# The scan phase of a two-block kernel: a loop over heads rewritten as staggered, unrolled periods

## The reference, cut to what matters

```python
def _gla_chunked(q, k, v, logf, s0):
    ...
    bc = jnp.cumsum(logf, axis=3)                       # within a chunk
    ref = bc[..., CHUNK // 2:CHUNK // 2 + 1, :]
    scores = jnp.einsum('bhnid,bhnjd->bhnij', q * jnp.exp(bc - ref), k * jnp.exp(ref - bc))
    scores = jnp.where(incl, scores, 0.0)
    o_intra = jnp.einsum('bhnij,bhnjv->bhniv', scores, v)
    q_dec = q * jnp.exp(bc)
    k_dec = k * jnp.exp(bc[..., -1:, :] - bc)
    tot = jnp.exp(bc[..., -1, :])
    def step(S, xs):                                    # over the chunks
        o_c = jnp.einsum('bhcd,bhdv->bhcv', qd_c, S)
        S = tot_c[..., :, None] * S + jnp.einsum('bhcd,bhcv->bhdv', kd_c, v_c)
    ...
# around it, per head: q = silu(q), f = lb + (1 - lb) * sigmoid(fx), logf = log(f), k = 1 - f,
# o = rmsnorm(o_forward + flip(o_backward)) * norm_w * silu(gate)
```

## Time and profile before

| | us |
|---|---|
| median of three executions | 5560.26 |
| profiled execution, its own time | 5562.48 |
| its span | 5560.7 |
| scan phase in it | 448.40 |
| TensorE busy in the scan phase | 232.37 |
| VectorE busy in the scan phase | 252.79 |
| ScalarE busy in the scan phase | 171.10 |

### The profile page before, as it was taken

How to read it: one execution, slowest core, us unless ns; L and a number is a source line. 1 busy time by engine, 2 the same in 40 slices (tenths; PEclk the granted TensorE clock), 3 DMA queues, 4 the chain that set the end, 5 groups by cost and what they waited for, 6 DMA issues and landing times. The chain is left out here.

```text
span 5560.7 us, 68785 instructions
## 1 busy us (share of the span) xinstructions
PE 4873.5 (88%) x24244; PEld 3969.3 (71%) x24244; DVE 3176.1 (57%) x5103; ACT 2093.4 (38%) x2408; POOL 110.1 (2%) x167
## 2 busy tenths in 40 slices
PE   8927799999999389997999954568999999899998
PEld 3923487778777278885899944433788888788887
DVE  0062498889888622232888746522787666344444
ACT  1001277776767201112555534310333444322222
POOL 1000100000000100000000011000000000000000
PEclk9557899999999789998999955579999999999999
DMA  8402599999999432344011011032434445566663
GB/s 337 151 30 89 228 369 366 365 368 370 367 363 368 154 134 106 109 145 124 29 35 35 15 43 42 30 108 92 148 126 132 168 171 198 193 210 192 192 195 122
DMA packets 256044, 976.04 MB, mean 176 GB/s; under 512 B 27060, under 2 KB 63492, under 8 KB 202212
## 3 DMA queue, kind: packets, MB, share of 16 engines
q1 hardware_dynamic: 248516, 923.74, 46.4%
q0 software_dynamic: 7392, 50.50, 2.2%
HBM read 799.87 MB, written 174.28 MB: 175 GB/s over the span
## 5 line engine op out<-in xcount | busy, mean ns | idle before, releaser
L84 PE MATMUL peer_bank<-peer_t_high,peer_high 128*128 128x512 f32 x2176 | 856.4, 394 | 49.3 <-DVE peer_low L2662 35.3
L86 PE MATMUL peer_bank<-peer_t_high,peer_low 128*128 128x512 f32 x2176 | 849.7, 390 | 0.0
L85 PE MATMUL peer_bank<-peer_t_low,peer_high 128*128 128x512 f32 x2176 | 848.2, 390 | 0.0
L2662 DVE TENSOR_TENSOR peer_low<-peer_raw,peer_high 128x1024 fp32r<-128x1024 f32 x272 | 332.4, 1223 | 621.8 <-ACT peer_high L3003 621.8
L1076 DVE TENSOR_TENSOR moe_low<-moe_raw,moe_high 128x2048 fp32r<-128x2048 f32 x256 | 574.4, 2285 | 55.9 <-ACT moe_high L984 53.0
L84 PEld LDWEIGHTS peer_bank<-peer_t_high,peer_high 128*128 128x128 f32 x2176 | 409.8, 188 | 133.0 <-issue 50.5
L984 ACT ACTIVATE moe_high<-moe_raw 128x2048 fp32r<-128x2048 f32 x256 | 478.0, 1905 | 2.6 <-DMA moe_raw<-w_gate_up 2.6
L86 PEld LDWEIGHTS peer_bank<-peer_t_high,peer_low 128*128 128x128 f32 x2176 | 409.5, 188 | 86.7
L3003 ACT ACTIVATE peer_high<-peer_raw 128x1024 fp32r<-128x1024 f32 x272 | 287.1, 1056 | 489.6 <-PE peer_bank L86 481.5
L85 PEld LDWEIGHTS peer_bank<-peer_t_low,peer_high 128*128 128x128 f32 x2176 | 410.0, 188 | 83.6
L1081 DVE TENSOR_TENSOR moe_low<-moe_raw,moe_high 128x2048 fp32r<-128x2048 f32 x128 | 292.9, 2288 | 66.8 <-ACT moe_high L989 66.8
(11 more groups left out here) (537 smaller groups left out, 9356.0 us busy)
## 6 DMA issues: line engine op xcount, KB each, us to landing
moe_raw<-w_gate_up SPq DMA_DIRECT2D x256, 1024.0 KB, 6.8
moe_raw<-w_down SPq DMA_DIRECT2D x128, 1024.0 KB, 7.4
peer_raw<-expert_u SPq DMA_DIRECT2D x128, 512.0 KB, 3.7
peer_raw<-expert_v SPq DMA_DIRECT2D x128, 512.0 KB, 3.6
hidden<-peer_gelu SPq DMA_DIRECT2D x128, 256.0 KB, 2.1
gate_matrix<-peer_stage SPq DMA_DIRECT2D x8, 4096.0 KB, 12.1
peer_stage<-gate_matrix SPq DMA_DIRECT2D x32, 1024.0 KB, 7.5
peer_stage<-hidden SPq DMA_DIRECT2D x128, 256.0 KB, 3.4
```

Of the source, the lines that this page charges most:

```text
L84: pe.matmul(out, wh, xh, start=start, stop=False)
L85: pe.matmul(out, wh, xl, start=False, stop=False)
L86: return pe.matmul(out, wl, xh, start=False, stop=stop)
L2662: v.tensor_tensor(low_part[:, slot], raw[:, slot], high[:, slot].bitcast(F32), ALU.subtract).then_inc(cut_low, 1)
```

## The change

In the input phase ScalarE's copies are unrolled, and those of the 40 tiles that the scan phase reads (two forget inputs, i, q, gate of the branch) write the 512 grid tokens in column order, reading PSUM with a stride of 64 elements. The scan phase has no such reordering left, nor any work of GpSimd after its start.

In the scan phase the loop is unrolled into periods p = -1 to 9. In period p the engines do three things in turns: the start of head p+1 (sigmoid, q, v, log, cumulative sums), the middle of head p (decays, scores, updates, states), and the end of heads p-1 (output, sum of squares, gate, logarithm) and p-2 (inv, o1, o2). Tiles q and v have two buffers. The tiles of the two directions lie in one tile with a direction axis, so that Sigmoid, Ln, e1 to e4, k, kd, ke, qe and qd are one instruction for both. The mask is a predicated copy of the whole bank (pt, `visible`), qd moves to VectorE (`queries`), and root and reciprocal give way to Ln (lno) and Exp (inv) on ScalarE. `Marks` is `Steps` with the head's number known when the code is made.

```diff
-            def copy_only(i, n, ps):
+            def in_order(tile, dst, src):
+
+                if tile // HEADS in (Z_FF // HEADS, Z_FB // HEADS, Z_I // HEADS, Z_QB // HEADS, Z_GB // HEADS):
+                    return by_columns(dst), src.rearrange("p (r w) -> p w r", w=GRID_W)
...
+                act.activation(*in_order(tile, out[:, n, 0:SEQ], bank[n % 2][0][:]), ACT.Copy).then_inc(half_taken, 1)
+                act.wait_ge(half_taken, tile + 1)
+                act.activation(out[:, n, SEQ:], bank[n % 2][1][:], ACT.Copy).then_inc(both.taken, 1)
...
-
-            def body(i):
-                for n in range(4):
-                    act.wait_ge(both.products, i * 4 + n + 1)
-                    need(act, z_stored[n], 16 * i)
-                    act.activation(out[:, n, 0:SEQ], bank[n % 2][0][:], ACT.Copy).then_inc(half_taken, 1)
-                    act.wait_ge(half_taken, i * 4 + n + 1)
-                    act.activation(out[:, n, SEQ:], bank[n % 2][1][:], ACT.Copy).then_inc(both.taken, 1)
-
-            rounds(act, BOTH // 4, body)
-            only.take(act, copy_only)
...
-        fz = [s.sb(f"fz{r}", [P, TOK]) for r in dirs]
+        fz = s.sb("fz", [P, 2, TOK])
...
+        q = [s.sb(f"q{n}", [P, SEQ]) for n in range(2)]
+        v = [s.sb(f"v{n}", [P, PAIRS, P]) for n in range(2)]
+        sg, k, lf, bc, dl, e4, kd = (s.sb(n, [P, 2, TOK]) for n in ("sg", "k", "lf", "bc", "dl", "e4", "kd"))
+        dm, e1, e2, e3, qe, ke, qd = (s.sb(n, [P, 2, SEQ]) for n in ("dm", "e1", "e2", "e3", "qe", "ke", "qd"))
...
+            def log_out(h):
+                TO.after(act, "sumsq", h)
+                VE.after(act, "o1", h - 1)
+                AO.mark("lno", h, act.activation(inv[:], ssb[:], ACT.Ln, scale=DK_SCALE ** 2, bias=eps[:]))
+
+            for p in PERIODS:
+                if head(p - 2):
+                    AO.after(act, "lno", p - 2)
+                    AE.mark("inv", p - 2, act.activation(inv[:], inv[:], ACT.Exp, scale=-0.5))
+                if head(p):
+                    decays(p, ("e4", "e2", "e1", "tot_f", "tot_b"))
+                    keys(p, 0)
+                    decays(p, ("e3",))
+                    keys(p, 1)
+                if head(p - 1):
+                    square_out(p - 1)
+                if head(p + 1):
+                    sigmoids(p + 1)
+                if head(p - 1):
+                    gates(p - 1)
+                if head(p + 1):
+                    values(p + 1)
+                    logs(p + 1)
+                if head(p - 1):
+                    log_out(p - 1)
...
+            def outputs(h):
+                VE.after(pe, "o1", h - 1)
+                AO.after(pe, "sq", h - 1)
+                VS.after(pe, f"s{NCH - 2}_b", h)
                 for r in dirs:
...
+                        pe.matmul(ob[:, c * P:(c + 1) * P], v[h % 2][:, c], pt[r][:, c], start=r == 0 and c == 0, stop=False,
                                   skip_group_check=True)
...
+                        last = pe.matmul(ob[:, part], state[r][:, c], qd[:, r, part], start=False, stop=r == 1,
                                          skip_group_check=True)
-            rounds(pe, HEADS, body)
+                TO.mark("out", h, last)
...
+            for p in PERIODS:
+                if head(p):
+                    turn_keys(p, 0)
+                    scores(p, 0)
+                if head(p - 1):
+                    outputs(p - 1)
+                if head(p):
+                    turn_keys(p, 1)
+                    updates(p, 0)
+                    scores(p, 1)
+                    updates(p, 1)
+                if head(p - 1):
+                    sums(p - 1)
+                if head(p + 1):
+                    turn_values(p + 1)
...
-            def body(h):
...
+            def lengths(h):
+                AG.after(ve, "sg", h)
+                VS.after(ve, "ke", h - 1)
+                VG.mark("k", h, ve.tensor_scalar(k[:], sg[:], lbm1[:, h:h + 1], oml[:, h:h + 1], ALU.mult, ALU.add))
...
-                    for b, (lo, part) in enumerate(windows[r]):
-                        rows = slice(lo, lo + 32)
-                        m = mask[r][rows, part].unsqueeze(1).to_broadcast([32, 4, part.stop - part.start])
-                        V.mark(f"pt{b}_{x}", ve.tensor_tensor(pt[r][rows, :, part], ptb[rows, :, part], m, ALU.mult))
...
-                V.mark("meansq", ve.tensor_scalar(root[:], ssb[:], DK_SCALE ** 2, RMS_EPS, ALU.mult, ALU.add))
-                A.after(ve, "root", h)
-                V.mark("inv", ve.reciprocal(inv[:], root[:]))
...
+                    order = (lambda a: a) if r == 0 else (lambda a: a[:, ::-1])
+                    AG.after(ve, "lf", h)
+                    AS.after(ve, "e3", h - 1)
+                    VG.mark(f"bc_{x}", h, ve.tensor_tensor_scan(order(bc[:, r]), keep[:], order(lf[:, r]), 0.0, ALU.mult, ALU.add))
...
+            def decayed(h):
+                AS.after(ve, "e4", h)
+                VG.after(ve, "k", h)
+                TS.after(ve, "tk1_b", h - 1)
+                VS.mark("kd", h, ve.tensor_tensor(kd[:], k[:], e4[:], ALU.mult))
...
+            def visible(h, r):
+                x = R[r]
+                TS.after(ve, f"scores_{x}", h)
+                TO.after(ve, "out", h - 1)
+                VS.mark(f"pt_{x}", h, ve.copy_predicated(pt[r][:], mask[r][:].unsqueeze(1).to_broadcast([P, 4, P]).bitcast(U32), ptb[:]))
+
+            def queries(h):
+                AS.after(ve, "e3", h)
+                TO.after(ve, "out", h - 1)
+                VS.mark("qd", h, ve.tensor_tensor(qd[:], q[h % 2][:].unsqueeze(1).to_broadcast([P, 2, SEQ]), e3[:], ALU.mult))
...
-            rounds(ve, HEADS, body)
...
+            for p in PERIODS:
+                if head(p - 2):
+                    norm(p - 2)
+                if head(p):
+                    decayed(p)
+                if head(p - 2):
+                    gated(p - 2)
+                if head(p):
+                    visible(p, 0)
+                    queries(p)
+                    states(p, 0)
+                    visible(p, 1)
+                if head(p + 1):
+                    lengths(p + 1)
+                if head(p):
+                    states(p, 1)
+                if head(p + 1):
+                    sums_of_logs(p + 1)
```

More of the change, by code:

```diff
@@ new lines, in sigmoids, with values, logs @@
+                AG.mark("q", h, act.activation(q[h % 2][:], qz[:], ACT.Silu))
+            def values(h):
+                TO.after(act, "out", h - 2)
+                for n, (a, b) in enumerate(spans):
+                    TG.after(act, f"tv{n}", h)
+                    AG.mark(f"v{n}", h, act.activation(v[h % 2][:, a:b], tr[n][:, 0:b - a], ACT.Copy))
+            def logs(h):
+                act.wait_ge(lbs, 3)
+                VG.after(act, "bc_b", h - 1)
+                AG.after(act, "sg", h)
+                AG.mark("lf", h, act.activation(lf[:], sg[:], ACT.Ln, scale=oml[:, h:h + 1], bias=lb[:, h:h + 1]))
@@ new lines, in gates @@
+            def gates(h):
+                act.wait_ge(loaded["g"], 16 * (h + 1))
+                VE.after(act, "o2", h - 1)
+                AO.mark("gate", h, act.activation(gate[:], gz[:], ACT.Silu))
+            def log_out(h):
[22 more added lines that the diff above has]
+                    log_out(p - 1)
@@ new lines, in turn_keys, with turn_values @@
+                        last = pe.transpose(tr[n][:, c - a], kd[:, r, c * P:(c + 1) * P], ident[:])
+                    TS.mark(f"tk{n}_{R[r]}", h, last)
+            def turn_values(h):
+                pe.wait_ge(loaded["i"], 16 * (h + 1))
+                for n, (a, b) in enumerate(spans):
+                    AS.after(pe, f"kdt{n}_b", h - 1)
+                    for c in range(a, b):
+                        last = pe.transpose(tr[n][:, c - a], iz[:, c * P:(c + 1) * P], ident[:])
+                    TG.mark(f"tv{n}", h, last)
@@ new lines, in scores @@
+            def scores(h, r):
+                x = R[r]
+                VS.after(pe, "qe", h)
+                if r:
+                    VS.after(pe, "pt_f", h)
+                else:
+                    VS.after(pe, "pt_b", h - 1)
+                for c in range(4):
+                    for lo, part in windows[r]:
+                        last = pe.matmul(ptb[lo:lo + 32, c, part], ke[:, r, c * P + lo:c * P + lo + 32],
+                                         qe[:, r, c * P + part.start:c * P + part.stop], start=True, stop=True)
+                TS.mark(f"scores_{x}", h, last)
@@ new lines, in updates @@
+            def updates(h, r):
+                x = R[r]
+                AS.after(pe, f"kdt1_{x}", h)
+                AG.after(pe, "v1", h)
+                if r:
+                    VS.after(pe, f"s{NCH - 2}_f", h)
+                else:
+                    VS.after(pe, f"s{NCH - 2}_b", h - 1)
+                for n in range(2):
+                    if n:
+                        TS.after(pe, f"kv0_{x}", h)
+                    for c in range(n, NCH, 2):
```

(17 more changed lines are left out.)

305 lines of the change are left out of this document (130 added, 175 removed).

## The result

| kernel | median, us | lowest to highest | runs | ratio to before [95%] |
|---|---|---|---|---|
| before | 5560.92 | 5558.92 to 5561.85 | 4 | |
| changed | 5470.8 | 5466.23 to 5480.48 | 4 | 0.9841 [0.9824, 0.9858] |
| predicted | 5475.0 | 5440 to 5520 | | |

The changed kernel is 90 us faster, 4 us more than forecast. The first view is the table of stretches of the changed kernel (columns as in the earlier trace rows). Its rows are, in this order: the scan phase, its period 4, in that period the backward updates and then the stretch from within the outputs to the recurrence, and last period 0.

A forecast was written before the change was run, and what follows sets the result against it. Scan phase bound by a chain of waits through all engines, not by one engine: 19.3 + 35.3 + 252 + 56 = 362.6 us against 448.4, so 5560.3 - 85.8 + 0.5 = 5475 us, range 5440 to 5520.

The forecast's parts named there:

- e4: ScalarE in the scan phase: one decay instruction for both directions, 1536 elements, priced at 1.5 us.
- start, to the end of the first sums: Scan phase start: first lf left at 11 us, then lf 1.65 and cumulative sums 6.6, together 19.3 us.
- periods 1 to 6: Scan phase: 48.3 us a period at 1.2 GHz, less 2.6, 2.8 and 0.8 for the clock, gives 42.
- end: Period 7 without sums: its outputs done at 45.8 us, then 10 to the end of the phase: 56 us.
- input phase: Strided copies of 40 tiles near 1.1 us, hidden except once at the change between lists: 0.5 us more.
- The chain: Scan phase bound by a chain across engines and heads; v and Ln of head p+1 stand behind all of head p.
- The waits named: Expected idle: TensorE some 14 us before kd's transposes, VectorE about 5 before the first state copy and 3 before sums.
- The clock: TensorE rises to 2.4 GHz within or just after the outputs, is down again for backward kv: 42 us a period.
- the two rivals on it: Clock down all through: 5517 us, chance 0.17; clock up for most of each period: 5412 to 5441, chance 0.14.
- the period nearer 35.6: Scan period walked with TensorE at 2.4 GHz from the outputs on: 35.6 us, taken as the skill page's rule.
- The prices: Instruction times in the scan phase from earlier rows: kd 1.75, sigmoid 1.5, Ln 1.65, pt 0.73 us.
- The rival in which this made the kernel slower: Input phase: strided PSUM reads make ScalarE the bound; with 12 us a copy 5675 us, chance 0.02.

The follow-up runs named there:

- the waits filled: Changed kernel plus unread matmuls of 128x512 in TensorE's waits, ten before the forward transposes and three before the backward updates: 5438.82 us.
- six extra matmuls: Kernel with the outputs behind the updates plus 6 unread matmuls of 128x512 before the forward transposes of each head: 5413.91 us.

## Why the prediction was right

Its terms, measured in the profiled execution (a period's length is the same from kd's transposes as from the end of the sums, 3.4 us earlier):

| term | predicted | measured |
|---|---|---|
| start, to the end of the first sums | 19.3 | 19.2 |
| period 0 | 35.3 | 35.8 |
| periods 1 to 6 | 6 x 42 = 252 | 250.3 (43.2, 43.8, 40.8, 40.7, 40.9, 40.9) |
| end | 56 | 53.5 |
| phase | 362.6 | 358.8 |
| input phase | +0.5 | none |

**The chain.** It was the right one, and the experiments moved two of its links: v ahead of the last updates took 15 to 19 us off, and with the outputs out of the way of the forward updates as well it was 47 to 51 (by the two medians of the changed kernel). VectorE's own 23 us a period never became the bound. The waits named are there: TensorE 13.5 us for kd (about 14), VectorE 1.95 before the first state copy (about 5, the part that was too large, since kv came earlier at 2.4 GHz) and 2.38 before the sums (about 3).

**The clock.** It rose within the outputs and was down for the backward updates, as forecast, and in this profile the two rivals on it fell: it was neither down throughout nor up for most of a period (0.61 on the mean). Inside that step the sizes were off. The outputs, taken at 8.5 us, took 9.0 and 9.6 in periods 1 and 2, where the clock rose late in them, and 6.6 to 6.8 in periods 3 to 6. The backward kv, taken at 5.1 although the same sentence had the clock down for it, took 5.88 like every other kv at 1.2 GHz. So two periods were over 43 and four under 41, and that their sum lies within 2 us of 6 x 42 is partly luck. The step itself had luck too: with only qd moved to GpSimd, three periods in one execution took 47.9 us, near the 48.3 of the rival in which the clock stays down. state x qd at 2.4 GHz, for which there was no row, takes 1.73 to the next start; 1.8 was used.

The prediction has the period nearer 35.6 by the rule of the Trainium skill ("TensorE: Matmul & The Clock Gate", Part 1). That reads only half of it: the same part has the clock back at its low level after idling, and the trace agrees, since it is at 0.50 behind the waits for kd (13.5 us) and for the recurrence (3.73). So 35.6 is a walk at full clock and not what the page gives. As such a walk it is good: with the waits filled the one period that kept the high clock nearly throughout took 35.2 us. Four others took 37.4 to 37.9; in period 3 the sum of squares and v's transposes are 2.07 and 1.46 us instead of 1.12 and 0.82, 1.6 us of the difference.

**The prices** held: kd of 1536 1.76 us (1.75), e4 1.48 (1.5), sigmoid 1.49 (1.5), Ln 1.67 (1.65), pt 0.73. For Ln the slope of its own rows gives 1.75 (1.94 less a fixed part of 0.19), so the 1.65 is a lucky figure. Ln starts 0.02 us behind its table load again (3433.07 + 1.28 = 3434.35, and 3434.37), and the load 0.02 us behind the copies of v, so the drain of 1.38 us in the Trainium skill ("ScalarE: Activation LUTs", What ACT_TABLE_LOAD costs) isn't there in this case either.

**The start and the end.** The phase came out 3.8 us short, 2.5 of them at the end. The forecast has the backward kv of period 7 at 31 us, which its own terms don't give (34.9 - 2.6 - 2.8 - 0.8 = 28.7); it was there at 27.6. Against that, from the last square to the end of the phase it was 11.3 us for 10: the gate's load and Silu and the load for Ln lie in it, and the forecast had left them out.

**The input phase.** The strided read costs nothing: 24 of the first 40 copies and 16 of the other 48 are strided, and both groups are as long as the unstrided ones in the earlier trace rows. Of the first 40 the shortest took 597 ns and the longest 598. The copies near 1.1 us that the prediction expected aren't there.

```profile
L1404 ACT ACTIVATE zin_outx<-zin_tokens 128x512 f32<-128x512 f32 x48 | 28.7, 599 | 241.5 <-PE zin_tokens L86 241.5
...
L1397 ACT ACTIVATE zin_out<-zin_tokens 128x512 f32<-128x512 f32 x40 | 23.9, 598 | 298.1 <-PE zin_context L86 298.1
```

The rival in which this made the kernel slower rested on a strided sigmoid from another memory, and falls with it.

**What the forecast didn't say.** It gave one sum for a change with parts of opposite sign. Unstaggered, the rest of the change is 25 us slower than before, most of it the wait for the last state that now stands in front of v x pt; the stagger hides it and gives 115 us. The walk is right without that wait, because it holds for the staggered order alone.

## What to carry to other kernels

Look for what stands in an in-order queue in front of the instruction that starts the next round's chain. Moving such work brought 15 to 51 us here, while merging instructions and taking 63 us of busy time off VectorE brought nothing without the stagger. Staggering rounds pays only as far as the queue's order lets the next round go ahead.

When several pieces of work are gathered into one function, look at where its waits land. A wait that only the second piece needs cost 1.8 us a direction in front of the first, and the comparison of the order of instructions didn't show it.

Price TensorE's work at the level of the clock that the rows beside it have, and expect that level to differ between executions; the same 24 matmuls were 3.26 or 5.88 us within one period.

The fastest order found without extra matmuls is the one with the outputs behind the updates, 5419.8 us, 51 less than the changed kernel; with six extra matmuls it was not distinguishable from that.

## What the runs showed of the hardware

- The granted clock did not rise merely because TensorE was busy. It stayed at 0.50 for 24 us with 23.62 us of work in them; in the changed kernel it rose within the outputs in every period from 1 on, and from period 4 to 6 once more behind the backward updates (v's transposes 1.05 to 1.15 us, before that 1.49). It fell in waits, as in the 3.73 us before the backward updates, but with TensorE at work too: with six extra matmuls, in period 5, it fell within the forward updates (granted 1.00 until 3415 us, 0.50 from 3416; kv 4.43), after waits of no more than 1.31 us. What decides was not measured and stays open.
- One kernel had periods of 28.7 and 36.0 us by turns, with the same instructions in both and a granted clock of 0.88 and 0.67.
- ScalarE's copy of 128x512 from PSUM took 0.598 us a tile with a stride of 64 elements as without it; the strided sigmoid of the same size took 1.07 where 0.61 is the price by the slope of the others.
